# Two expert lanes of 64 rows become one of 96 and one of 32, in three strips of the array

## What is computed

```python
_, eidx = lax.top_k(sel, TOP_K)                      # 8 of 64 experts
gate = take_along_axis(scores, eidx) / sum * 2.5
xb = h[tb]                                           # the rows of one block of one expert
hid = silu(xb @ w_exp_gate[e]) * (xb @ w_exp_up[e])  # 1024 -> 256
out = (hid @ w_exp_down[e]) * gb[:, None]            # 256 -> 1024
routed = zeros_like(h).at[tok].add(outs)
```

## Time and profile before

| | us |
|---|---|
| median of 3 runs | 1289.78 |
| lowest, highest | 1287.50, 1293.22 |
| the profiled execution, its own time | 1285.27 |
| its span | 1283.1 |
| PE busy | 1175.4 (92%) |
| DVE busy | 434.7 (34%) |
| ACT busy | 214.5 (17%) |
| POOL busy | 137.1 (11%) |

### The profile page before, as it was taken

How to read it: one execution, slowest core, us unless ns; L and a number is a source line. 1 busy time by engine, 2 the same in 40 slices (tenths; PEclk the granted TensorE clock), 3 DMA queues, 4 the chain that set the end, 5 groups by cost and what they waited for, 6 DMA issues and landing times.

```text
span 1283.1 us, 19182 instructions
## 1 busy us (share of the span) xinstructions
PE 1175.4 (92%) x5813; PEld 493.3 (38%) x5813; DVE 434.7 (34%) x1122; ACT 214.5 (17%) x437; POOL 137.1 (11%) x155
## 2 busy tenths in 40 slices
PE   2899999998779999799999999999999999899964
PEld 1334444475424444233333333333333333333322
DVE  2103123056413447712323333233222232233257
ACT  2200100245400112011111111111111111111101
POOL 2000000000002001001111111111111111111100
PEclk9899999999879999799999999999999999899978
DMA  9965442198077000589899888887999999998596
GB/s 322 404 240 212 173 131 70 75 326 273 1 219 265 33 21 1 209 311 413 341 342 375 320 349 318 355 328 287 411 375 420 371 382 416 358 378 333 180 362 264
DMA packets 65772, 351.62 MB, mean 274 GB/s; under 512 B 11591, under 2 KB 11591, under 8 KB 32278
## 3 DMA queue, kind: packets, MB, share of 16 engines
q1 hardware_dynamic: 48766, 309.93, 63.4%
q0 software_dynamic: 15680, 37.03, 7.5%
q10 hardware_dynamic: 1240, 3.78, 0.8%
HBM read 336.03 MB, written 34.13 MB: 288 GB/s over the span
## 4 chain that ended last, share of the span: by engine, by line
PE 48%; issue 6%; DVE 6%; DMA 5%; SPq 2%; ACT 1%; POOL 0%; DVEq 0%; ACTq 0%; POOLq 0%
PE psum L1359 25%; PE psum L1385 11%; DMA sb_stream<-w_exp_up 5%; PE psum L1333 3%; PE psum L1823 2%; PE psum L1836 2%; PE psum L1365 1%; PE psum L1373 1%; PE psum L1309 1%; SPq L721 1%; DVE sb_work L2067 1%; PE psum L1349 1%; SPq L1284 0%; DVE sb_x L2045 0%; SPq L1408 0%
## 5 line engine op out<-in xcount | busy, mean ns | idle before, releaser
L1359 PE MATMUL psum<-sb_stream,sb_convg 128*64 128x512 f32 x1664 | 373.5, 602 | 12.0 <-DMA sb_stream<-w_exp_up 10.5
L1359 PEld LDWEIGHTS psum<-sb_stream,sb_convg 128*64 128x64 f32 x1664 | 116.8, 139 | 224.9 <-issue 223.4
L1385 PE MATMUL psum<-sb_stream,sb_hbuf 128*64 128x512 f32 x832 | 190.0, 598 | 0.0
L1495 POOL DMA_INDIRECT expert_rows<-sb_attn,sb_row x52 | 52.2, 1004 | 528.7 <-DVE sb_token L1319 276.1
L1782 DVE TENSOR_TENSOR sb_hbuf<-psum,sb_hbuf 128x256 f32<-128x256 f32 x53 | 22.5, 424 | 213.1 <-ACT sb_hbuf L1552 213.1
L1385 PEld LDWEIGHTS psum<-sb_stream,sb_hbuf 128*64 128x64 f32 x832 | 55.1, 136 | 95.4 <-issue 89.3
L634 PE MATMUL psum<-sb_hT,sb_stream 128*128 128x512 f32 x192 | 87.4, 612 | 3.0 <-DMA sb_stream<-w_in 3.0
L1810 DVE TENSOR_SCALAR sb_attn<-psum,sb_now_gate 128x512 f32<-128x512 f32 x52 | 39.1, 751 | 149.0 <-PE psum L1385 149.0
L698 PE MATMUL psum<-sb_stream,sb_hT 128*128 128x512 f32 x192 | 84.5, 596 | 0.0
L1552 ACT ACTIVATE sb_hbuf<-psum 128x256 f32<-128x256 f32 x53 | 20.3, 383 | 373.3 <-PE psum L1359 372.0
L1333 PEld LDWEIGHTS psum<-sb_cst,sb_work 128*128 128x128 f32 x424 | 51.3, 194 | 43.0 <-issue 43.0
(11 more groups left out here) (323 smaller groups left out, 1031.3 us busy)
## 6 DMA issues: line engine op xcount, KB each, us to landing
sb_stream<-w_exp_gate SPq DMA_DIRECT2D x65, 1024.0 KB, 7.1
sb_stream<-w_exp_up SPq DMA_DIRECT2D x65, 1024.0 KB, 10.5
sb_stream<-w_exp_down SPq DMA_DIRECT2D x65, 1024.0 KB, 10.6
sb_stream<-w_ada SPq DMA_DIRECT2D x12, 2048.0 KB, 18.5
sb_stream<-expert_rows SPq DMA_DIRECT2D x7, 2048.0 KB, 19.3
sb_stream<-w_in SPq DMA_DIRECT2D x6, 2048.0 KB, 15.1
sb_stream<-cache_k SPq DMA_DIRECT2D x8, 1024.0 KB, 12.0
sb_stream<-cache_v SPq DMA_DIRECT2D x8, 1024.0 KB, 14.7
```

What stands on the lines that cost most here:

```text
L1359: last = pe.matmul(psum[lo:lo + LANE, 0, :].rearrange("p (a n) -> p a n", a=2), xT[:, k, lo:lo + LANE], gu[j][:, k, :, :], start=(k == 0), ...
L1385: last = pe.matmul(psum[lo:lo + LANE, 4 + n, :], hidT[:, k, lo:lo + LANE], dn[j][:, k, n * 512:(n + 1) * 512], start=(k == 0), stop=(k == 1))
L1495: pool.indirect_dma_start(expert_rows, bass.IndirectOffsetOnAxis(ap=row[:, u, :], axis=0), out[:, u, :], None, bounds_check=last_expert_ro ...
```

## The change

The two lanes get 96 rows (MAIN) and 32 rows (SIDE). The array is used in strips, since a product's columns are 32, 64 or 128: rows 0 to 63 and 64 to 95 are two strips of the wide lane with the same weights, rows 96 to 127 the narrow lane. Every product of a lane is now issued for three strips.

Experts are counted in blocks of 96. An expert of at most 64 rows is small; it may go to the narrow lane, in one or two blocks of 32. Small experts are taken in their order as long as the running sum of (blocks of 96 + blocks of 32) is at most the number of all blocks of 96. Each lane has its own two queues, and the number of trips is half the longer lane's blocks. The largest number of trips that any data could need is now TRIPS = 54, and ROUNDS = 18.

Because the table of blocks is larger it lies in `wr` (the router's weights, read before). The constants grow from 808 to 953 columns. To make room for them `sp0` goes, and group 0 of the sample scores is also written into `k_sb`, so the wait for the stores comes before `read_scores(0)`.

```diff
-LANE = 64
-LANES = P // LANE
+MAIN, SIDE = 96, 32
+LANES = 2
+LANE_AT, LANE_W = (0, MAIN), (MAIN, SIDE)
+STRIPS = ((0, 64, 0), (64, 32, 0), (96, 32, 1))
 QUEUES = 2 * LANES
-MAXB = (NTOK * TOPK + NE * (LANE - 1)) // LANE
-TRIPS = -(-MAXB // QUEUES)
+APART = 1000
+TRIPS = -(-((NTOK * TOPK + NE * (MAIN - 1)) // MAIN) // 2)
...
+    c[:, C_ROUND2:C_ROUND2 + P] = SIDE * (p[None] // 2)
...
-        sp0 = tmp("s_probs", [P, SK])
-        sp_of = (sp0[:, :], k_sb[:, :, :].rearrange("p t n -> p (t n)")[:, 0:SK])
+        sp_of = [k_sb[:, :, :].rearrange("p t n -> p (t n)")[:, g * SK:(g + 1) * SK] for g in range(2)]
...
                     if e == UNITS:
                         v.wait_ge(masks_in, 16)
+                        v.wait_ge(stored, 4 * 16)
                         read_scores(0)
-                v.wait_ge(stored, 4 * 16)
                 read_scores(1)
...
             v.wait_ge(s["blk_ok"], LANES * b + LANES)
-            v.tensor_tensor(oh[:, u, :, :].rearrange("p t (j n) -> p t j n", j=LANES),
-                            lane[:, tl * P:(tl + 1) * P].rearrange("p (j n) -> p j n", j=LANES).unsqueeze(1).broadcast_to([P, NT, LANES, LANE]),
-                            blk[:, u, :, :].unsqueeze(3).broadcast_to([P, NT, LANES, LANE]), ALU.is_equal).then_inc(s["oh_ok"], 1)
+            for j in range(LANES):
+                lo, w = LANE_AT[j], LANE_W[j]
+                v.tensor_tensor(oh[:, u, :, lo:lo + w], lane[:, tl * P + lo:tl * P + lo + w].unsqueeze(1).broadcast_to([P, NT, w]),
+                                blk[:, u, :, j:j + 1].broadcast_to([P, NT, w]), ALU.is_equal).then_inc(s["oh_ok"], 1)
...
             for t in range(NT):
-                for j in range(LANES):
-                    last = pe.matmul(psum[j * LANE:(j + 1) * LANE, 6, 0:9], oh[:, u, t, j * LANE:(j + 1) * LANE],
+                for lo, w, j in STRIPS:
+                    last = pe.matmul(psum[lo:lo + w, 6, 0:9], oh[:, u, t, lo:lo + w],
                                      pick[:, u, j, t, :], start=(t == 0), stop=(t == NT - 1))
...
             for k in range(KC):
-                for j in range(LANES):
-                    lo = j * LANE
-                    last = pe.matmul(psum[lo:lo + LANE, 0, :].rearrange("p (a n) -> p a n", a=2), xT[:, k, lo:lo + LANE],
+                for lo, w, j in STRIPS:
+                    last = pe.matmul(psum[lo:lo + w, 0, :].rearrange("p (a n) -> p a n", a=2), xT[:, k, lo:lo + w],
                                      gu[j][:, k, :, :], start=(k == 0), stop=(k == KC - 1))
...
                 for k in range(2):
-                    for j in range(LANES):
-                        lo = j * LANE
-                        last = pe.matmul(psum[lo:lo + LANE, 4 + n, :], hidT[:, k, lo:lo + LANE],
+                    for lo, w, j in STRIPS:
+                        last = pe.matmul(psum[lo:lo + w, 4 + n, :], hidT[:, k, lo:lo + w],
                                          dn[j][:, k, n * 512:(n + 1) * 512], start=(k == 0), stop=(k == 1))
...
-                    for n in range(1, -(-NTOK // LANE)):
-                        step(v.scalar_tensor_tensor(nblk, cnt, float(n * LANE), nblk, ALU.is_gt, ALU.add))
-                    single, few, many, starts, stops = (sel[:, n, :] for n in range(NT))
-                    of_many, total, last_block = (gsum[:, n:n + 1] for n in range(3))
-                    step(v.tensor_scalar(single, nblk, 1.5, None, ALU.is_lt))
-                    step(v.tensor_tensor(few, nblk, single, ALU.mult))
-                    step(v.tensor_tensor(many, nblk, few, ALU.subtract))
-                    ends = running(erun[0], erun[1], 96, many)[..., 32:]
-                    step(v.tensor_tensor(starts, ends, many, ALU.subtract))
-                    step(v.tensor_copy(of_many, ends[:, NE - 1:NE]))
-                    ends = running(erun[0], erun[1], 96, few)[..., 32:]
-                    step(v.tensor_tensor(few, ends, few, ALU.subtract))
-                    step(v.tensor_tensor(total, of_many, ends[:, NE - 1:NE], ALU.add))
-                    step(v.scalar_tensor_tensor(few, few, of_many, single, ALU.add, ALU.mult))
-                    step(v.tensor_tensor(many, starts, single, ALU.mult))
-                    step(v.tensor_tensor(starts, starts, many, ALU.subtract))
-                    step(v.tensor_tensor(starts, starts, few, ALU.add))
-                    step(v.tensor_tensor(stops, starts, nblk, ALU.add))
-                    step(v.tensor_scalar(last_block, total, -1.0, None, ALU.add))
-                    step(v.tensor_scalar(first, starts, float(LANE), 1.0, ALU.mult, ALU.add))
+                    for n in range(1, -(-NTOK // MAIN)):
+                        step(v.scalar_tensor_tensor(nblk, cnt, float(n * MAIN), nblk, ALU.is_gt, ALU.add))
+                    small_one, thin, weight, moved, at_main = (sel[:, n, :] for n in range(NT))
+                    at_side, both, stops, starts = (selm[:, n, :] for n in range(4))
+                    all_main, span_, last_block, longest = (gsum[:, n:n + 1] for n in range(4))
+                    step(v.tensor_scalar(small_one, cnt, 2 * SIDE + 0.5, None, ALU.is_lt))
+                    step(v.scalar_tensor_tensor(thin, cnt, SIDE + 0.5, nblk, ALU.is_gt, ALU.add))
+                    step(v.tensor_tensor(weight, thin, nblk, ALU.add))
+                    step(v.tensor_tensor(weight, weight, small_one, ALU.mult))
+                    step(v.tensor_reduce(all_main, nblk, AX.X, ALU.add))
+                    ends = running(erun[0], erun[1], 96, weight)[..., 32:]
+                    step(v.scalar_tensor_tensor(moved, ends, all_main, small_one, ALU.is_le, ALU.mult))
+                    lanes_of = ra[:, 0:LANES, :]
+                    step(v.tensor_tensor(both, nblk, moved, ALU.mult))
+                    step(v.tensor_tensor(lanes_of[:, 0, :], nblk, both, ALU.subtract))
+                    step(v.tensor_tensor(lanes_of[:, 1, :], thin, moved, ALU.mult))
+                    ends = running(run[0][:, 0:LANES, :], run[1][:, 0:LANES, :], 96, lanes_of)[..., 32:]
+                    step(v.tensor_tensor(at_main, ends[:, 0, :], lanes_of[:, 0, :], ALU.subtract))
+                    step(v.tensor_tensor(at_side, ends[:, 1, :], lanes_of[:, 1, :], ALU.subtract))
+                    n_main, n_side = ends[:, 0, NE - 1:NE], ends[:, 1, NE - 1:NE]
+                    step(v.tensor_tensor(longest, n_main, n_side, ALU.max))
+                    step(v.scalar_tensor_tensor(span_, n_side, float(APART), n_main, ALU.add, ALU.subtract))
+                    step(v.scalar_tensor_tensor(last_block, cst[:, C_LANE:C_LANE + 1], span_, n_main, ALU.mult, ALU.add))
+                    step(v.tensor_tensor(both, at_main, moved, ALU.mult))
+                    step(v.tensor_tensor(at_main, at_main, both, ALU.subtract))
+                    step(v.tensor_tensor(at_side, at_side, moved, ALU.mult))
+                    step(v.tensor_scalar(first, at_main, float(MAIN), 1.0, ALU.mult, ALU.add))
+                    step(v.scalar_tensor_tensor(first, at_side, float(SIDE), first, ALU.mult, ALU.add))
+                    step(v.tensor_tensor(starts, at_main, at_side, ALU.add))
+                    step(v.scalar_tensor_tensor(starts, moved, float(APART), starts, ALU.mult, ALU.add))
+                    step(v.tensor_tensor(both, lanes_of[:, 0, :], lanes_of[:, 1, :], ALU.add))
+                    step(v.tensor_tensor(stops, starts, both, ALU.add))
                     step(v.tensor_tensor(ra, psum[:, 2, 0:NT * NE].rearrange("p (t e) -> p t e", t=NT),
                                          first.unsqueeze(1).broadcast_to([P, NT, NE]), ALU.add))
                     step(v.tensor_tensor(ra, ra, mask, ALU.mult))
                     step(v.tensor_scalar(gpos, ra, -1.0, None, ALU.add))
-                    step(v.tensor_scalar(cnt[:, 0:TRIPS], cst[:, C_TRIP:C_TRIP + TRIPS], total, None, ALU.is_lt))
+                    step(v.tensor_scalar(cnt[:, 0:TRIPS], cst[:, C_TRIP:C_TRIP + TRIPS], longest, None, ALU.is_lt))
                     step(v.tensor_reduce(tripf, cnt[:, 0:TRIPS], AX.X, ALU.add))
-                    step(v.scalar_tensor_tensor(lane.rearrange("p (q n) -> p q n", q=QUEUES),
-                                                cst[:, C_CQ:C_CQ + QUEUES].unsqueeze(2).broadcast_to([P, QUEUES, LANE]), tripf,
-                                                cst[:, C_IOTA:C_IOTA + LANE].unsqueeze(1).broadcast_to([P, QUEUES, LANE]),
-                                                ALU.mult, ALU.add))
+                    for tl in range(2):
+                        for j in range(LANES):
+                            lo, w = tl * P + LANE_AT[j], LANE_W[j]
+                            if tl:
+                                step(v.scalar_tensor_tensor(lane[:, lo:lo + w], tripf.broadcast_to([P, w]), float(w),
+                                                            cst[:, C_IOTA:C_IOTA + w], ALU.mult, ALU.add))
+                            else:
```

(28 more changed lines are left out.)

2 lines of the change are left out of this document (removed).

## The result

The changed kernel takes 2011.55 us (median of 4 runs, 2006.0 to 2012.18) against 1288.64 for the kernel before (4 runs, 1284.8 to 1293.22), a ratio of 1.560 with an interval of 1.557 to 1.564. The profiled execution took 2006.0 us, its span 2004.2. The forecast was 2012.

The account below looks back on a forecast made before the run. PE was taken to set the pace, busy 92%, with DMA close behind. Loop 651, empty rounds 66 and 6 before the loop gave +723 on 1285.3, so 2008, plus 4.5 for the median: 2012 us, range 1820 to 2185.

Parts of the forecast that it names:

- Width and not columns: PE in a block: 64-wide and 32-wide strips take turns despite disjoint columns, 1.98 us a k step against 0.86; chance 0.80.
- Size of a block: Expert block on PE: gate/up 15.84, down 7.92, list 1.25 us, so a block goes from 12.29 to 26.54 us.
- Loop: Loop start to the end of the last-but-two block's down product: 1291 us against 639.7, +651.
- late weights: Waits for expert weights in the loop, part of some 17 us lost before, vanish as 65 sets have twice the time.
- Number of blocks: Expert loop: 50 blocks in 25 trips instead of 52 in 26; two block times go, 24.6 us at the old price.
- Empty rounds: SP's loop end: nine rounds without trips instead of two delay the sample rows' load, seven more of 9.5 us, +66.
- the rival in which they grow cheap: SP's tail: skipped code kept at hand over nine equal rounds, strips overlapping; 1277 us, faster by 1%, chance 0.04.
- Before the loop: Ahead of the expert loop: more DVE queue steps, three lists and mask products on PE, larger constants; together +6 us.
- At nothing: Priced at zero: `who` in the loop, the earlier wait for the stores, and the table's new place.
- strips that overlap: Rival for PE's blocks: unequal strips stream together and the empty rounds show; +53, 1343 us, slower by 4%, chance 0.13.
- the long tail: SP's empty rounds between its last weight load and the sample rows' load: +66 us, bounds 55 to 72.
- overlap without the tail: Rival: unequal strips stream together and SP's empty rounds add nothing; 1277 us, faster by 1%, chance 0.04.

Follow-up runs that it names:

- experiments 1: The kernel before, with the second of its two 64-row lanes issued as two strips of 32 columns: 2010.22 us, ratio 1.557.
- experiment 2: The changed kernel with four strips of 32 columns, three for the wide lane and one for the narrow: 1448.37 us, ratio 1.122.
- experiment 4: The changed kernel with all k steps of the 64-wide strip first, then those of the two 32-wide strips: 1861.68 us, ratio 1.442.
- experiment 5: The changed kernel with ROUNDS set to 9 instead of 18: 1959.38 us, ratio 1.520.
- the hint: The changed kernel on four strips of 32, PE's loop told at each round's top that its closing branch goes back: 1355.3 us, ratio 1.051.
- experiment 9: The changed kernel with four strips of 32, back-branch hints on PE's and SP's loops, and the number of rounds computed from the trips: 1281.51 us, ratio 0.9953.

## Why the prediction was right

- **Width and not columns.** The step on which all hung, that strips of unequal width take turns though their columns are disjoint, was a choice between two cases the rows left open, at 0.80. It held (the loads of after; experiments 1, 2, 4). "TensorEngine Tiling (Array Packing)" in the Trainium skill, Key Properties, has the change of tiling mode drain the engine; after and experiment 4 agree, also where the strips share no column. Its parallel tiles hold, by experiment 2, for strips of one width.
- **Size of a block.** 15.84 + 7.92 + 1.25 against 15.88 + 7.94 + 1.20; block 26.54, as said. The four half-passes added up (0.48 + 0.52 + 0.46 + 0.52) because each is the same exposed load and drain seen elsewhere in the trace of before.
- **Loop.** +651 forecast. The first block starts at 556.61 and the down product of the last but two ends at 1847.21: 1290.6 against 1291, +650.9. The late weights vanished, as said.
- **Number of blocks.** L1363 has 2400 records, 50 x 48.
- **Empty rounds.** +66 forecast, and 92.4 us against 26 measured. The skips stayed at 2 us over nine rounds, and SP's queue carries five packets for each round added, so the rival in which they grow cheap is out; experiment 5 shows that the sample load waited for them.
- **Before the loop.** +6 was too much: the loop starts 1.6 us later. The queues on DVE cost about 2.5 as said; but the start moves from run to run (553.2 to 560.3 in the six traces with the lanes of before, 556.6 to 562.2 in the six with the new ones), so the rest of this term cannot be read. Behind the sample load the new kernel takes 2 us more (64.6 for 62.6), which I had at nothing. The sum is 1.6 + 650.9 + 66.5 + 2.0 = 721.1 us (rounded terms), 2004.2 less 1283.1. That 2012 was forecast and 2011.55 measured is closer than the working deserves: 4.4 us too much ahead of the loop and 2 too little behind it partly cancel, and the four runs alone span 6 us.
- **At nothing.** The wait for the stores and `who` in the loop do not show: every block is as long as its products.
- **The rivals' sums.** For strips that overlap I had 1343 with the long tail; such strips took 1448 (experiment 2). The term that lacked is the 93 us that the hint takes away, fetching at each jump back and the lower clock behind it; no row of before could show it, since the body of before fetches nothing after its first rounds. With the hint it is 1355. The 1277 of overlap without the tail compares with 1281.5 of experiment 9.

## What to carry to other kernels

Price a narrower or wider matmul strip by what its neighbours in time are: here strips of one width streamed beside each other for free, and one strip of another width made the two widths take turns at full price, plus some 0.14 us for every change. Before widening the bound of a loop with conditional bodies, find which engine walks the empty rounds last, here 9.5 us each on the engine that issues the next load, or compute the bound. When a body is made of more and smaller instructions, look at the engine's instruction packets and its waits for issue at the jump back, and try a hint on the branch. And price a wait of PE with what follows it: behind each of those waits the granted clock was 0.50 for a while, which cost nearly half as much again as the waits (29 us beside 64).

## What the runs showed of the hardware that I had not expected

- PE's loop body has a size from which every round fetches instructions anew: about 1220 instructions a round fetched nothing more once inside (23 packets in all), about 1570 fetched 9 packets of 16 KB a round (101 packets, 1.65 MB in all). In the round shown that cost 7.2 us at the jump, 3.2 after five records, and some 3.5 by a clock of 1.2 GHz behind them.
- A hint at the top of the body took the packets from 92 to 25 and 93 us off the kernel, some 29 of them by the clock.
- Empty rounds on SP bring in instructions too: its queue carries 65 packets before and 100 after, 5 for each added round, 55 with two fewer, and 14 with hint and computed rounds.
- Four strips of 32 cost no more than two of 64 in the middle of a trip (7.07 and 3.64 us in the timeline), but 0.3 us at a branch, where PE waits for issue.
